# Hybrid attention trunk on eight cores: interleaved query tiles and all keys on every core, against four programs with contiguous token ranges

## What is computed

```python
def hybrid_layer(x, mem, ...):
    h = rms_norm(x, g_in)
    (c_q, c_kv, k_pe, z_mla, q_swa, k_swa, v_swa, z_swa, q_mem, z_mem) = split_cols(h @ w_in, IN_SIZES)
    y_mla = mla_attention(c_q, c_kv, k_pe, ...) * jax.nn.silu(z_mla)
    y_swa = swa_attention(q_swa, k_swa, v_swa, sinks, rel_table) * jax.nn.silu(z_swa)
    y_mem = memory_attention(q_mem, rms_norm(mem, g_mem), w_mem_kv) * jax.nn.silu(z_mem)
    y = jnp.concatenate([y_mla, y_swa, y_mem], axis=-1) @ w_out
    return x + y
```

## Time and profile before

| what | value |
|---|---|
| median of 3 runs | 859.26 us (859.23 to 859.91) |
| the profiled execution: span of its slowest core | 856.2 us, core 0 |
| spans of the eight cores | 840.5 to 856.2 us |
| PE, DVE, ACT busy on core 0 | 785.2, 505.0, 419.9 us |
| DMA, all queues of core 0 | 95.52 MB |
| HBM read, written | 116.49 MB, 8.39 MB |

### The profile page before, as it was taken

The page is one execution under the profiler, slowest core; times in us unless marked ns, Lnnn a source line. Parts: engine busy times, 40 slices in busy tenths (PEclk is TensorE's granted clock), DMA queues, the critical chain, the costliest instruction groups (busy, mean ns, idle before and its releaser), DMA issues.

```text
span 856.2 us, 12303 instructions; the slowest of 8 cores (840.5 to 856.2 us)
## 1 busy us (share of the span) xinstructions
PE 785.2 (92%) x4540; PEld 394.3 (46%) x4540; DVE 505.0 (59%) x654; ACT 419.9 (49%) x513; POOL 21.4 (2%) x41
## 2 busy tenths in 40 slices
PE   2779997989899899978989999999999999899994
PEld 0245553444454333323445555555555555344442
DVE  1736765776775487766965566565665755233433
ACT  1348656521004367754546676766757678122221
POOL 3200000000000000000000000000000000000000
PEclk9989998999999999989999999999999999999998
DMA  9999959346465222287490000000000029941212
GB/s 166 264 178 189 176 150 162 109 125 233 148 219 224 98 100 99 100 166 191 136 182 4 1 2 1 2 1 1 1 2 2 1 69 212 269 164 74 91 58 98
DMA packets 18303, 95.52 MB, mean 112 GB/s; under 512 B 1858, under 2 KB 6082, under 8 KB 9220
## 3 DMA queue, kind: packets, MB, share of 16 engines
q0 software_dynamic: 8016, 35.13, 23.1%
q1 hardware_dynamic: 10228, 59.60, 19.5%
HBM read 116.49 MB, written 8.39 MB: 146 GB/s over the span
## 4 chain that ended last, share of the span: by engine, by line
PE 69%; DMA 14%; DVE 8%; ACT 4%; issue 3%; POOL 0%; DVEq 0%; ACTq 0%; SPq 0%; POOLq 0%
PE psd L584 16%; PE psd L1020 12%; PE psd L340 7%; PE psd L917 6%; PE psd L918 6%; PE psd L931 6%; DMA hown_57<-xu 5%; DMA wo_157<-wo 4%; PE psd L862 3%; PE psd L876 3%; DMA stage_87<-wti 3%; PE psd L838 3%; PE psd L959 1%; DMA hrot_58<-xu 1%; DMA wst_79<-wkv 1%
## 5 line engine op out<-in xcount | busy, mean ns | idle before, releaser
L584 PE MATMUL psd<-hown_57,ring_89 128*128 128x512 bf16 x288 | 68.9, 398 | 3.8 <-DVE kvnT_53 L212 2.1
L584 PE MATMUL psd<-hown_57,ring_91 128*128 128x512 bf16 x288 | 64.3, 379 | 2.1 <-DVE zrt_116 L209 1.4
L917 PE MATMUL psd<-Qn_125,Kb_121 128*128 128x512 bf16 (+2 forms) x192 | 59.5, 326 | 0.7 <-ACT Kb_121 L206 0.7
L917 PE MATMUL psd<-Qn_126,Kb_122 128*128 128x512 bf16 (+2 forms) x192 | 59.5, 326 | 0.0
L918 PE MATMUL psd<-Qp_128,kpeT_54 128*128 128x512 bf16 (+2 forms) x192 | 57.8, 326 | 0.0
L918 PE MATMUL psd<-Qp_127,kpeT_54 128*128 128x512 bf16 (+2 forms) x192 | 57.8, 326 | 0.0
L584 PEld LDWEIGHTS psd<-hown_57,ring_89 128*128 128x128 bf16 x288 | 28.8, 102 | 42.5 <-issue 13.2
L584 PEld LDWEIGHTS psd<-hown_57,ring_91 128*128 128x128 bf16 x288 | 27.5, 98 | 36.9 <-issue 5.0
L206 ACT ACTIVATE pmb_133<-psd 128x1024 bf16<-128x1024 f32 x24 | 24.6, 1024 | 31.4 <-PE psd L918 9.9
L340 PE MATMUL psd<-hown_57,wkv_63 128*128 128x512 bf16 x112 | 30.3, 433 | 8.4 <-DMA hown_57<-xu 5.0
L584 PE MATMUL psd<-hown_57,ring_92 128*128 128x512 bf16 x160 | 36.0, 379 | 1.0 <-DVE zrt_115 L209 1.0
(11 more groups left out here) (376 smaller groups left out, 1533.7 us busy)
## 6 DMA issues: line engine op xcount, KB each, us to landing
stage_87<-wti SPq DMA_DIRECT2D x18, 1024.0 KB, 5.7
stage_88<-wti SPq DMA_DIRECT2D x10, 1024.0 KB, 5.2
stage_88<-wmk SPq DMA_DIRECT2D x8, 1024.0 KB, 5.6
hown_57<-xu POOLq DMA_DIRECT2D x4, 512.0 KB, 16.3
hown_57<-xu POOLq DMA_DIRECT2D x2, 1024.0 KB, 34.7
hrot_58<-xu POOLq DMA_DIRECT2D x2, 1024.0 KB, 27.6
hrot_59<-xu POOLq DMA_DIRECT2D x2, 1024.0 KB, 35.0
hrot_60<-xu POOLq DMA_DIRECT2D x2, 1024.0 KB, 35.9
```

Source lines behind the costliest of these rows:

```text
L584: cp("dve", cqf.t[:, c, hs], pf(b, 0, 512), [PS[b]], [cqf])
L917: def mm(e):
```

## The change

The four cores of a batch element get four different programs. `ROLES` gives each a first tile and a number of tiles, 11, 8, 7 and 6, and `ROLE_OF` says which core has which. A core computes latents and keys only up to the end of its own range (`units_of`: own units first, the rest after them). Each engine loads the role from memory into a register and branches to its part (`pick`). The 64 rows of mask are gone: the rotary product has 64 rows, two heads are handled together (a pair), the second head's rotary operands lie in partitions 64 to 127, and the one chunk that must not be seen in a diagonal tile is set to zero by a memset on POOL after the Exp. The rotary keys of two units are computed side by side in two halves of the array's columns (`kpe`), and the banded values are made as keys are, then transposed by matmul. The row sums of a pair are gathered on VectorE in a float32 accumulator (`sums`), closed by one matmul of ones per head. Both output banks (6 and 7) now belong to one block of queries, copied out by VectorE at its end. The order is no longer written out: generators for the keys' stage, the own projections, the memory and the banded attention and the first pair's keys are merged by clocks that run at fixed rates (`merge`), and buffers are placed by lifetime (`layout`). Weights are fetched three chunks ahead. The DMA requests for the last two parts of `w_out` are issued in `output`, after the attention's last instructions. The diff, cut to what the text speaks of:

```diff
...
+ROLES = ((0, 11), (11, 8), (19, 7), (26, 6))
+ROLE_OF = (0, 3, 1, 2)
...
+def units_of(role):
+    s, n = ROLES[role]
+    own = split4(s, n)
+    rest = split4(0, s)
+    if rest:
+        rest = [rest[-1]] + rest[:-1]
+    return own, rest
...
+    def merge(self, streams):
+        clock = [0.0] * len(streams)
+        live = [True] * len(streams)
+        idle = 0
+        while any(live):
+            for i in sorted((i for i in range(len(streams)) if live[i]), key=lambda i: clock[i]):
+                try:
+                    c = next(streams[i][0])
+                except StopIteration:
+                    live[i] = False
+                    c = 0
+                    break
+                if c is None:
+                    continue
+                clock[i] += c / streams[i][1]
+                self.job_done()
...
+        for kc in range(16):
+            for i, u in enumerate(us):
+                lst.append((self.pf(b, 0, self.T[u], 64 * i, 64 * i + 64), self.wkv[:, kc, 512:576], self.xa(u, kc),
+                            kc == 0, kc == 15, self.T[u] / len(us)))
+        c = self.mm(lst, reads, [self.PS[b]], "kpe")
...
+        def kg(u):
+            T = self.T[u]
+            kv, kvp = self.kvn[u]
+            k = self.ps2()
+            c = self.mm([(self.pf(k + h, 0, T), wk[:, kc, p * 512 + h * 128:p * 512 + h * 128 + 128], kv[:, kc, :], kc == 0,
+                          kc == 1, T) for h in range(2) for kc in range(2)], [wkp, kvp], [self.PS[k], self.PS[k + 1]], "kg")
+            o = sum(self.T[:u])
+            self.cp(self.KV[p][0][:, :, o:o + T], self.pair(k, T), [self.PS[k], self.PS[k + 1]], [self.KV[p][1][u]], 2 * T,
+                    "act")
...
+        def vg(u):
+            T = self.T[u]
+            kv, kvp = self.kvn[u]
+            n = T // 128
+            k = self.ps2()
+            lst = []
+            for t in range(n):
+                for kc in range(2):
+                    lst.append((self.pf(k + t // 2, (t % 2) * 256, (t % 2) * 256 + 256), kv[:, kc, t * 128:t * 128 + 128],
+                                wk[:, kc, p * 512 + 256:p * 512 + 512], kc == 0, kc == 1, 256))
+            c = self.mm(lst, [wkp, kvp], [self.PS[k], self.PS[k + 1]], "vg")
...
+        DLY = 3
+        outq = []
+        for m in range(0, n_ + DLY + 3, 2):
+            for n in (m, m + 1):
+                if n < n_:
+                    if n % per == 0:
+                        for j in jobs:
+                            j()
+                        p = n // per
+                        jobs = self.up_jobs(p + 1) if p < 3 else []
+                        nj = len(jobs)
+                        if p == 3:
+                            self.load_out()
+                    self.front(steps[n], n % 2)
+            for n in (m - DLY - 1, m - DLY):
+                if 0 <= n < n_:
+                    self.back(steps[n])
+            k = (m % per) + 2
+            while jobs and (nj - len(jobs)) < nj * k / (per - 4.0):
+                jobs.pop(0)()
+            self.job_done()
...
+        for u, tile, o, c0, w, _ in st["ps"]:
+            o_ = sum(self.T[:u])
+            kcol = slice(tile * 128, tile * 128 + 128)
+            lc = tile * 128 - o_
+            qs = slice(qs0 + c0, qs0 + c0 + w)
+            kt_parts += [Kp[u], self.kp[u][1]]
+            for h in range(2):
+                a.append([self.pf(k + h, o, o + w), K[:, h, kcol], qn[:, h, qs], h, w])
+            for h in range(2):
+                rs = slice(64 * h, 64 * h + 64)
+                b_.append([self.pf(k + h, o, o + w), self.kp[u][0][rs, lc:lc + 128], qp[rs, qs], h, w])
+        seq = b_ + a if flip else a + b_
+        seen = set()
+        lst = []
+        nl = len(seq)
+        for i, (out, l, r, h, w) in enumerate(seq):
+            half = seq[i] in b_
+            lst.append((out, l, r, h not in seen, i >= nl - 2, w / 2 if half else w))
+            seen.add(h)
+        rd = list(dict.fromkeys(kt_parts)) + [qnp[st["b"]], qpp[st["b"]]]
+        self.mm(lst, rd, [self.PS[k], self.PS[k + 1]], "front")
+        pb, pbp = P.new("pmb", [128, 2, 512], BF16)
+        self.act(AF.Exp, pb[:, :, 0:cols], self.pair(k, cols), [self.PS[k], self.PS[k + 1]], [pbp], 2 * cols,
+                 scale=MLA_SCALE)
+        self.rel(k, k + 1)
+        for u, tile, o, c0, w, dg in st["ps"]:
+            if dg:
+                P.op("pool", lambda e, o=o: e.memset(pb[64:128, :, o:o + 64], 0.0), [], [pbp], 0.2)
+        st["pb"] = (pb, pbp)
+        self.sums(st)
...
+        def into(src, sp, lo, w, c0):
+            if not used[0]:
+                used[0] = True
+                assert lo == 0 and c0 == 0
+                self.cp(a[:, :, 0:w], src[:, :, 0:w], [sp], [ap], 2 * w)
+            else:
+                self.tt(ALU.add, a[:, :, c0:c0 + w], a[:, :, c0:c0 + w], src[:, :, lo:lo + w], [sp, ap], [ap], 2 * w)
+        if st["whole"]:
+            lv[0].append((pb, pbp))
+            if len(lv[0]) == 2:
+                (x, xp), (y, yp) = lv[0]
+                lv[0] = []
+                t, tp = P.new("p2", [128, 2, cols], BF16)
+                self.tt(ALU.add, t[:, :, :], x[:, :, 0:cols], y[:, :, 0:cols], [xp, yp], [tp], 2 * cols, True)
+                lv[1].append((t, tp))
+            if len(lv[1]) == 2:
+                (x, xp), (y, yp) = lv[1]
+                lv[1] = []
+                self.tt(ALU.add, x[:, :, :], x[:, :, :], y[:, :, :], [xp, yp], [xp], 2 * cols, True)
+                into(x, xp, 0, cols, 0)
+            st["wc"] = cols
+            self.wcols[key] = cols
+        else:
+            self.rest_of(key, lv, into)
+            per = self.fold_acc(key, a, ap, W, used)
+            for u, tile, o, c0, w, _ in st["ps"]:
+                into(pb, pbp, o, w, c0)
+        if st["last"]:
+            self.rest_of(key, lv, into)
+            self.fold_acc(key, a, ap, W, used)
+            h, hp = P.new("accb", [128, 2, W], BF16)
+            self.cp(h[:, :, :], a[:, :, 0:W], [ap], [hp], 2 * W)
+            self.accb[key] = (h, hp)
...
+        for i, (u, tile, o, c0, w, _) in enumerate(st["ps"]):
+            for h in range(2):
+                lst.append((self.pf(6 + h, c0, c0 + w), V[:, tile, h * 128:h * 128 + 128], pb[:, h, o:o + w],
+                            st["first"] and i == 0, st["last"] and i == len(st["ps"]) - 1, w))
+        rd = list(dict.fromkeys(Vp[x[0]] for x in st["ps"])) + [pbp]
+        self.mm(lst, rd, [self.PS[6], self.PS[7]], "back")
+        if st["last"]:
+            W = self.T[bq]
+            o, op = P.new("oc", [128, 2, W], F32)
+            self.cp(o[:, :, :], self.pair(6, W), [self.PS[6], self.PS[7]], [op], 2 * W)
+            self.soon(1, lambda: self.close(p, bq, o, op))
...
+        self.mm([(self.pf(k + i, 0, W), self.ones, h[:, i, :], True, True, W) for i in range(2)], [self.onesp, hp],
+                [self.PS[k], self.PS[k + 1]], "sum")
+        r, rp = P.new("rim", [128, 2, W], F32)
+        self.act(AF.Ln, r[:, :, :], self.pair(k, W), [self.PS[k], self.PS[k + 1]], [rp], 2 * W)
+        self.rel(k, k + 1)
+        self.act(AF.Exp, r[:, :, :], r[:, :, :], [rp], [rp], 2 * W, scale=-1.0)
+        self.tt(ALU.mult, o[:, :, :], o[:, :, :], r[:, :, :], [op, rp], [op], 2 * W)
+        t, ps = self.gA[p]
+        us = slice(self.O0[bq], self.O0[bq] + W)
+        self.tt(ALU.mult, t[:, :, us], o[:, :, :], t[:, :, us], [op, ps[bq]], [ps[bq]], 2 * W)
...
+    def output(self):
+        P = self.P
+        for i in range(2, 4):
+            self.wo.append(P.new("wo", [128, 16, 512], BF16))
+            P.dma("pool", self.wo[i][0][:, :, :].rearrange("p a b -> p (a b)"), self.dr["wo"][i], writes=[self.wo[i][1]],
+                  mb=4, what="wo")
+        gf, gfp = P.new("gfin", [128, D], F32)
+        P.dma("sp", gf[:, :], self.dr["gfin"][:, :], writes=[gfp], what="gfin")
...
+        for u in range(1, nu):
+            own = u < self.no
+            T = self.T[u]
+            if u + 1 < nu and u + 1 not in self.x:
+                self.fetch(u + 1)
+            self.squares(u, self.x[u][0], self.xp(u), T)
+            p = self.ps2()
+            yield self.group(u, 0, p)
+            yield self.group(u, 128, p + 1)
+            c = self.stat(u, T)
+            s2, s2p = self.latent_a(u, p)
+            yield c
+            if own:
+                yield from self.swa_kv(u, 0, 128 * (self.s > 0) + self.O0[u])
+            elif u == self.no:
+                yield from self.swa_kv(u, T - 128, 0)
+                self.pred = True
+            if u % 2 == 1:
+                yield self.kpe([u - 1, u])
+            elif u == nu - 1:
+                yield self.kpe([u])
+            yield self.latent_b(u, p, s2, s2p)
+            if u == self.no - 1:
+                self.own_done = True
+        if not self.rest:
+            self.pred = True
+        self.kv_end = True
...
+        for _ in range(3):
+            self.load_w()
+        self.consts()
+        kv = self.kv_stream()
```

(24 more changed lines are left out.)

1916 lines of the change are left out of this document (1042 added, 874 removed).

## The result

The changed kernel takes 1189.27 us (median of 3 runs, 1188.76 to 1191.29) against 859.26: 1.385 times as long, with an interval of 1.382 to 1.388. The forecast was 810. The sign was wrong, and the range of 757 to 852 missed by 337 us.

A forecast was written before the change was run, and what follows sets the result against it. PE was taken to bound the old kernel, VectorE the 11-tile role's new attention. That role's head, units, projections, attention, output and branching gave 807 us of span, plus 3 around it: 810 us, range 757 to 852.

The forecast's parts named there:

- step 3: First role, the rest before attention after units 1 and 2: 346 us, bounds 325 and 365, ending at 439.
- streams that hold each other: Rival: automatic buffer placement makes engines wait for each other before and in the first role's attention; 890 us, chance 0.10.
- Step 1: First role's head, until unit 1 of x has landed: 60 us, between 52 and 63.
- Step 2: First role, units 1 and 2 on PE: 33 us, done at 93.
- Step 4: First role's attention: 188 us, bounds 166 and 208, ending at 627.
- VectorE binds: First role's attention is bound by VectorE: 166 us of it against 116 of PE and about 102 of ACT.
- Step 5: First role's output: 152 us, plus 15 waiting for w_out and a tail of 11, ending at 805.
- Step 6: Reading the role and branching at the start: 2 us, giving a span of 807.
- the 756 forecast for the 7-tile core: Whole span of the 7-tile role: some 5 us more than the 751 of its neighbour, the last role.
- PE's counts: PE's work per role from columns streamed, 216 ns per 512: together 636, 597, 620, 617 us against 753 before.
- The rotary pairs: In attention scores, two 64-row rotary products run side by side as one unit of 0.216 us; a run costs 0.11 more.
- The tests that I named: Forecast wrong if the 11-tile core is not last, its attention under 150 or over 215 us, or PE below 0.85 in projections.

The follow-up runs named there:

- e14_v_on_act: All helpful edits together, plus ACT instead of VectorE evicting the values made during attention in the 11- and 8-tile roles: 930.34 us, ratio 1.086 to the kernel before.
- e4_consts: Changed kernel with the small constants' DMAs and conversions moved behind the keys' first units: 1164.84 us.
- e9_lead_123: Changed kernel with fold before eviction, spaced small buffers, late constants, and one folded chunk in reserve only in the 8-, 7- and 6-tile roles: 1009.37 us.
- e12_deeper: As e9_lead_123, with second halves of gates two jobs later and of memory or banded pieces two pieces behind: 968.3 us.
- e11_no_sums: Changed kernel with fold-first, reserve, spacing and late constants, without latent attention's row sums (output wrong): attention 176, 299, 211, 275 us instead of 223, 327, 269, 324.

## Why the prediction was wrong

**The step that failed is step 3**, the rest before attention: 346 us for the first role, bounds 325 to 365, and 529 measured; on the 7-tile core, which ended last, attention began at 681 us, where 362 had been added up for its neighbour of 6 tiles. I scaled the waits of the kernel before to the length of the new stage. Those waits belonged to an order written out by hand with buffers placed by hand, and the change replaces both. They say nothing of the new order. Of the 529 us on core 0 PE was idle for 155: 35.1 for banded probabilities from ACT, 34.9 for the weights of the heads' queries, 21.5 for the memory's transposes, 17.3 for the last gates, 12.2 for folds, and smaller ones; and it was busy for 374 us where 325 were counted. On core 3 the folds were the largest, 161.7 us. The diff held much of what was needed: where `fold_w` stands relative to the eviction, how many units share a chunk, what `layout` may reuse, where `consts` stands. For one chunk on a two-unit core, its list reads: eviction, fold, eviction, fold, then matmuls. That is one fold of 1.2 us and an eviction that PE must wait for, about 2.3 us for most chunks, 52 us together. The other 110 us, in nine long waits, come with what else stands ahead of the fold, in eight of them passes of the keys' stage, and that takes more than one chunk's list to see.

**The price of the waits was mis-sized twice.** A wait costs its own length, and it costs clock. PE's busy time on core 3 was 772.5 us where 620 were counted; in e14_v_on_act, with fewer waits, it is 705. (The count itself is sound to a few us: the 3474 starts of the kernel before at 216 ns are 750, not 753.) My lower bound on PE's share had no term for that, although the row with 0.91 in the earlier trace rows showed it in small.

**The rival "streams that hold each other" had the right mechanism.** Buffers reused at once, Exp waiting for VectorE's last pass: the spaced layout shows it, 98 to 127 us where there is room, of which Exp's waits are about a half on core 3 and less on core 0. I gave it 890 us and 0.10. PE's share was priced at 0.80, and by starts it was 325 of 529, 0.61. It also was not alone: the fold, worth up to 106 us, the constants, 16 to 28, and w_out, 11 to 22, are losses of the same kind in other places, and one by one they sum. Against it I had put the shares of 0.94 and 0.98 of the hand order, which are the thing that the change throws away.

**Step 1**: head 60, and PE went on with unit 1 at 87.5 on core 0, after a wait of 31.6 us for its square sums. The landing of x was sized well: unit 1 was there at about 55 on core 3. That SP's weights and bias are asked for at once was not so; on core 3 their requests left at 42.6 to 53.4 us. What I missed is that the constants' conversions stand ahead of unit 1 on VectorE's list and their transfer behind the weights on SP's. In e4_consts core 3 starts 30 us earlier.

**Step 2**: 46 for 33 on core 0, with a wait of 16.9 for square sums in between. The keys were done at 134, not 93.

**Step 4**: attention 188, bounds 166 to 208, measured 251. The passes were right: VectorE was busy for 168.7 us where I had counted 166. The waits were not: 82 us instead of 22. Spacing takes 25 of them, the deeper delays 10 (about PE's waits of 6.7 and 2.7 us for the last gates in e9_lead_123), the evictions on ACT 18. And the conclusion that VectorE binds was half right: without its sums the stage is 47 us shorter, but it holds core 3 just as much, where its busy time says that it has room.

**Step 5** held: 186 for 178, with 13.1 us of waiting for w_out on core 0 where 15 stood. **Step 6** held for the first role only (below). PE's counts held: 155 us busy in the output at a clock of 0.93 for 152. The rotary pairs held, 0.54 us for four.

**The tests that I named** spoke plainly: the 11-tile core not last, its attention above 215, PE in its own projections below 0.85. All three came.

**What stays open.** Of the 434 us between 1190 and the 756 forecast for the 7-tile core the edits remove 266. The rest is not split up by a run. The waits left there in e14_v_on_act, by their rows, are for the keys' weights at the head (29.4 us), folds (27.3), the memory's transposes (21.2), the copy of the output banks (19.8), and the next pair's queries and values (40); and PE's busy time is 85 us over its count. On core 0, where the forecast was 807 us, 119 remain. Whether a full clock would come back with these gone was not tried.

## What to carry to other kernels

A count of each engine's work is a floor and says little of a schedule that a change makes anew: before trusting it, write down one period of each engine's list from the new code and look for who must wait for whom, above all for a producer's work placed behind an eviction or behind another stream's passes, and for a small buffer that reuses bytes just let go. The waits of a hand-made order are a property of that order and do not carry over. If a generated schedule is slow, spacing out buffer reuse is a cheap thing to try, since it changes addresses alone, and a second role or core with no room for it serves as its control.

## What the runs showed of the hardware

The way into a program by role costs more the deeper its branch lies. The first instruction of each program, a memset on POOL, in the timelines of cores 0, 2, 3 and 1, which take the first, second, third and last branch:

```profile
2.58 0.20 POOL L1198 MEMSET ones_r<- 128x128 bf16 x1 [1.87 <-issue]
...
3.07 0.20 POOL L1198 MEMSET ones_r<- 128x128 bf16 x1 [2.35 <-issue]
...
5.95 0.20 POOL L1198 MEMSET ones_r<- 128x128 bf16 x1 [5.24 <-issue]
...
12.66 0.20 POOL L1198 MEMSET ones_r<- 128x128 bf16 x1 [11.95 <-issue]
```

Before it stood at 1.06 us. So the price is 1.5, 2.0, 4.9 and 11.6 us, and within 1 us the same in e14_v_on_act (2.83, 3.17, 6.59, 11.76); I had 2 for all. The Trainium skill gives 108 ns for a compare and branch ("Advanced Engine Details and Errata", Control Flow Timing). Three of them would be a third of a microsecond, as an estimate from that figure, and the measurement decides: most of the price is something else. A queue of kind instruction (q14 on the pages) moves 0.26, 0.29, 0.38 and 0.38 MB on these four cores and 0.18 before, which makes the loading of code a candidate; no run here separates it.

The other is how much clock a wait costs. In the attention of core 3 PE was busy for 0.76, 0.83 and 0.92 of the time in the changed kernel, in e12_deeper and in e11_no_sums, and the granted clock was 0.90, 0.93 and 0.98. Between the first and the last of these PE's idle time in the stage fell from 88 to 22 us and its busy time from 285 to 253, for 1505 and 1506 matmuls. So 66 us of idle time taken away there made the stage 98 us shorter.
